# Two column units of a mixer output projection become one block with two seven-product chunk pairs

## The reference, cut to what matters

```python
oa = _mixer_sgu(za, ...)          # feature columns 0 to 511
ob = _mixer_shortconv(zb, ...)    # 512 to 1023
oc = _mixer_conformer(zc, ...)    # 1024 to 1535
od = _mixer_pool(zd, ...)         # 1536 to 2047
h = h + jnp.concatenate([oa, ob, oc, od], axis=-1) @ w_out[i]
y = _rms(h, norm_ffn_g[i])
h = h + (silu(y @ w_gate[i]) * (y @ w_up[i])) @ w_down[i]
y = _rms(h, norm_ple_g[i])
h = h + sigmoid(y @ w_ple_gate[i]) * (p[i] @ w_ple_proj[i])
```

## Time and profile before

| | |
|---|---|
| Median of 3 runs | 1378.77 us (1378.66 to 1379.81) |
| The profiled execution's own time | 1378.55 us |
| Its span | 1376.8 us |
| PE busy | 1370.2 us, 6169 matmuls |
| DVE, ACT, POOL busy | 1155.0, 885.1, 150.6 us |
| Moved by DMA | 352.94 MB, 256 GB/s mean |

### The profile page before, as it was taken

How to read it: one execution, slowest core, us unless ns; L and a number is a source line. 1 busy time by engine, 2 the same in 40 slices (tenths; PEclk the granted TensorE clock), 3 DMA queues, 4 the chain that set the end, 5 groups by cost and what they waited for, 6 DMA issues and landing times.

```text
span 1376.8 us, 16935 instructions
## 1 busy us (share of the span) xinstructions
PE 1370.2 (100%) x6169; PEld 1122.3 (82%) x6169; DVE 1155.0 (84%) x1332; ACT 885.1 (64%) x1181; POOL 150.6 (11%) x129
## 2 busy tenths in 40 slices
PE   9999999999999999999999999999999999999998
PEld 7888888888888888788888888888888887777887
DVE  6589986688999988899999889988766769886898
ACT  7476755576777555677756576756666656675564
POOL 2000010011111000110100011100000134430000
PEclk9999999999999999999999999999999999999999
DMA  9777658887999788899987889988987878889585
GB/s 331 251 211 212 203 164 277 278 248 242 292 283 261 229 260 257 252 270 266 281 267 249 252 252 244 281 292 236 326 297 274 279 240 259 254 271 300 193 251 170
DMA packets 183148, 352.94 MB, mean 256 GB/s; under 512 B 13106, under 2 KB 37934, under 8 KB 182937
## 3 DMA queue, kind: packets, MB, share of 16 engines
q1 hardware_dynamic: 160408, 291.66, 64.1%
q0 software_dynamic: 9568, 35.02, 13.0%
q10 hardware_dynamic: 13088, 25.18, 6.0%
HBM read 296.19 MB, written 27.31 MB: 235 GB/s over the span
## 4 chain that ended last, share of the span: by engine, by line
PE 96%; DVE 2%; DMA 1%; issue 1%; ACT 0%; POOL 0%; POOLq 0%; ACTq 0%; DVEq 0%
PE acc L2207 14%; PE acc L2209 14%; PE acc L2208 14%; PE acc L2388 13%; PE acc L2390 13%; PE acc L2391 13%; PE sp L2388 2%; PE tp L2390 2%; PE tp L2388 2%; PE tp L2391 2%; PE sp L2390 2%; PE sp L2391 2%; DMA wide<-w_raw 1%; PE acc L2269 1%; PE sp L2508 1%; DVE w_lo L1410 1%
## 5 line engine op out<-in xcount | busy, mean ns | idle before, releaser
L970 ACT ACTIVATE w_hi<-w_raw 128x1024 fp32r<-128x1024 f32 x451 | 472.0, 1056 | 298.5 <-PE acc L2209 192.1
L1410 DVE TENSOR_TENSOR w_lo<-w_raw,w_hi 128x1024 fp32r<-128x1024 f32 x429 | 519.8, 1226 | 137.1 <-ACT w_hi L970 134.5
L2207 PE MATMUL acc<-w_lo,hh 128*128 128x512 f32 x480 | 189.0, 394 | 0.0
L2209 PE MATMUL acc<-w_hi,hl 128*128 128x512 f32 x480 | 186.9, 389 | 0.0
L2208 PE MATMUL acc<-w_hi,hh 128*128 128x512 f32 x480 | 186.9, 389 | 0.0
L2388 PE MATMUL acc<-w_lo,yh 128*128 128x512 f32 x452 | 176.1, 390 | 0.0
L2391 PE MATMUL acc<-w_hi,yl 128*128 128x512 f32 x452 | 175.9, 389 | 0.0
L2390 PE MATMUL acc<-w_hi,yh 128*128 128x512 f32 x452 | 175.9, 389 | 0.0
L970 ACT ACTIVATE w_hi<-wide 128x1024 fp32r<-128x1024 f32 x108 | 114.4, 1060 | 72.8 <-DVE wide L1424 34.1
L1410 DVE TENSOR_TENSOR w_lo<-wide,w_hi 128x1024 fp32r<-128x1024 f32 x108 | 131.5, 1223 | 14.0 <-ACT w_hi L970 13.7
L2207 PE MATMUL acc<-w_lo,yh 128*128 128x512 f32 x352 | 137.4, 390 | 0.0
(11 more groups left out here) (333 smaller groups left out, 2225.8 us busy)
## 6 DMA issues: line engine op xcount, KB each, us to landing
w_raw<-in_w_gate SPq DMA_DIRECT2D x88, 512.0 KB, 5.7
w_raw<-in_w_up SPq DMA_DIRECT2D x88, 512.0 KB, 6.6
w_raw<-in_w_down SPq DMA_DIRECT2D x88, 512.0 KB, 6.5
w_raw<-in_w_in SPq DMA_DIRECT2D x64, 512.0 KB, 4.6
wide<-w_raw POOLq DMA_DIRECT2D x54, 512.0 KB, 6.0
w_raw<-in_swa_w_in ACTq DMA_DIRECT2D x48, 512.0 KB, 5.1
w_raw<-in_w_out SPq DMA_DIRECT2D x32, 512.0 KB, 5.8
w_raw<-in_w_ple_gate SPq DMA_DIRECT2D x32, 512.0 KB, 6.1
```

What stands on the lines that cost most here:

```text
L970: act.activation(w_hi[:, v % SPL], src, ACT.Copy).then_inc(hi_ready, 1)
L1410: dve.tensor_tensor(w_lo[:, v % SPL], src, w_hi[:, v % SPL].bitcast(F32), ALU.subtract).then_inc(lo_ready, 1)
L2207: pe.matmul(dst, xh[:, f, tk], w_lo[:, v % SPL, k], start=(f == 0), stop=False)
L2209: last = pe.matmul(dst, xl[:, f, tk], w_hi[:, v % SPL, k], start=False, stop=(f == CK * end + CK - 1))
```

## The change

The first two column units of `w_out` (units 12 and 13) become one `Block`, `MIXED_PAIR`, of 20 steps: twelve plain chunks and two quads (chunk pairs 0 and 1). With it come:

- a sum of the activations of those chunks, `whole_first` and `sum_h(0)`, in `tile[4]`, whose split takes the first of now five rounds of `h_sums` (all later rounds count one up);
- the four parkings of the projection of `p`, which now stand behind the loads 7, 8, 9 and 10 of the block, the first and the second of them around `move(T_OA)`, since `copy_tops` of the block is now the first of the program;
- other places for the residual's transposes, squares and `sum_y` in the last two units, which stay plain.

```diff
+MIXED_PLAN = plain(0, 2, 3) + plain(1, 2, 3) + plain(0, 6) + quad("g", 0) + plain(1, 6) + quad("g", 1) + plain(0, 7)
+MIXED_PLAN += plain(1, 7) + quad("u", 0) + quad("t", 0) + quad("s", 0) + quad("u", 1) + plain(0, 4) + quad("t", 1)
+MIXED_PLAN += quad("s", 1) + plain(0, 5) + plain(1, 4, 5)
+MIXED_AT = dict(whole=1, sums=4, sums_high=7, sums_low=8, m1=14, mix=18, mixed_gate=19, bank=19,
+                copied={6: [0], 7: [1]}, summed={0: 9, 1: 13})
...
+MIXED_PAIR = Block(OUT_UNIT, MIXED_PLAN, **MIXED_AT)
```

```diff
@@ SP
-            for j in range(NG):
+            b = MIXED_PAIR
+            for i, p in enumerate(b.loads):
+                role = int(p[0] == "u" or p[:2] == ("n", 1))
+                load(b.raw + i, wout_v, OUT_ROWS[p[-1]], CW * role)
+                if i == 7:
+                    put(T_OA)
+                if i == 8:
+                    fetch(T_OA)
+                if i in (7, 8, 9, 10):
+                    put_proj(i - 7)
+            for j in range(2, NG):
                 for c in range(8):
-                    if (j, c) == (0, 7):
-                        move(T_OA)
-                    if j >= 2 and c == 4:
+                    if (j, c) in ((2, 7), (3, 5)):
                         move(T_FFN + j - 2)
-                    if (j, c) in ((1, 3), (1, 7), (2, 7), (3, 3)):
-                        put_proj(((1, 3), (1, 7), (2, 7), (3, 3)).index((j, c)))
@@ ACT
+            b = MIXED_PAIR
+            for i in range(len(b.plan)):
+                for q in b.at["copied"].get(i, ()):
+                    copy_tops(b, q)
+                split_high(b.v0 + i)
...
+                if i == 3:
+                    turned_high(T_OA, hh[:, 8:12])
+                if i == b.at["sums_high"]:
+                    h_sums_to_high(0)
+                if i == b.at["m1"]:
+                    copy_m1(b)
@@ DVE
+            b = MIXED_PAIR
+            for i in range(len(b.plan)):
+                split_low(b.v0 + i)
...
+                if i == b.at["whole"]:
+                    whole_first()
...
+                if i == 3:
+                    turned_low(T_OA, hl[:, 8:12], hh[:, 8:12])
+                if i == b.at["sums"]:
+                    wait_half(dve, H_CN + 1)
+                    sum_h(0)
+                if i == b.at["sums_low"]:
+                    h_sums_to_low(0)
+                if i == b.at["mix"]:
+                    mix(b)
+                if i == b.at["mixed_gate"]:
+                    add_mixed_gate(b, 0)
+                if i == b.at["bank"]:
+                    add_bank(b, 0, 1)
...
+                    if (j, c) == (2, 0):
+                        wait_left(dve, OUT_UNIT)
+                        turn(T_FFN, columns(0))
+                        add_mixed_up(MIXED_PAIR, 1)
+                    if (j, c) == (2, 2):
+                        add_bank(MIXED_PAIR, 1, 2)
@@ PE
+            def before_mixed(i, p):
...
+                if p == ("n", 0, 6):
+                    pe.wait_ge(mix_ready, 2)
+                if p == ("g", 0):
+                    wait_half_left(pe, H_CN + 1)
+                    pe.wait_ge(oa_ready, 1)
+                if p == ("u", 0):
+                    pe.wait_ge(h_sums_low, 1)
+                if p == ("n", 0, 4):
+                    pe.wait_ge(turned_lo, T_OA + 1)
+            block(MIXED_PAIR, hh, hl, h_sums_hi, h_sums_lo, None, before_mixed)
```

More of the change, by code:

```diff
@@ L1127, in _, with copy_m1, h_sums_to_high @@
             take(PROJ_UNIT, wide_v[:, :, 0:CW], ACT.Copy, 1.0)
-            for j in range(NG):
+            def copy_m1(b):
+                act.wait_ge(used, b.split("g", b.quads[-1]) + 1)
+                if b is PAIR[0]:
+                    act.wait_ge(y_sums_low, 1)
+                act.activation(gates[:, 0], tp[0][:], ACT.Copy).then_inc(m1_copied, 1)
+            def h_sums_to_high(r):
+                act.wait_ge(h_sums, 4 * r + 4)
+                act.activation(h_sums_hi[:], h_wide(r), ACT.Copy).then_inc(h_sums_high, 1)
@@ new lines, in _ @@
+            b = MIXED_PAIR
[3 more added lines that the diff above has]
+                split_high(b.v0 + i)
+                if i < 3:
+                    take(PROJ_UNIT + 1 + i, wide_v[:, :, CW * (i + 1):CW * (i + 2)], ACT.Copy, 1.0)
+                if i == 2:
+                    wait_half_left(act, H_PO + 1)
+                    for h in range(2):
+                        wait_half(act, H_CN + h)
+                        for k in range(2):
+                            f = 2 * h + k
+                            last = act.activation(feat(6)[:, f], half_tile(H_CN + h)[:, k], ACT.Silu,
+                                                  bias=vec[:, V_LB + f:V_LB + f + 1],
+                                                  scale=vec[:, V_LG + f:V_LG + f + 1])
+                        last.then_inc(tp_left["a"], 1)
+                    wait_half_left(act, H_CN + 1)
+                    act.activation(hh[:, 12:16], feat(6), ACT.Copy).then_inc(mix_hi, 1)
+                if i == 3:
[4 more added lines that the diff above has]
+                    copy_m1(b)
@@ L1167, in hidden_high @@
                 turned_high(T_HID + m, hh[:, q:q + 4])
-            def copy_m1(b):
-                act.wait_ge(used, b.split("g", b.quads[-1]) + 1)
-                if b.no == 1:
-                    act.wait_ge(y_sums_low, 1)
-                act.activation(gates[:, 0], tp[0][:], ACT.Copy).then_inc(m1_copied, 1)
             def gate(m):
@@ new lines, in add_bank, with whole_first @@
+            def add_bank(b, d, after):
+                wait_unit(dve, b.unit + d % 2)
+                dve.wait_ge(mixed_added, after)
+                dve.tensor_tensor(columns(d), acc_pair[(b.unit + d) % 2][:], columns(d), ALU.add).then_inc(left["d"], 1)
+            def whole_first():
+                dve.tensor_tensor(tile[7][:], hh[:, 0:4].bitcast(F32).rearrange("p k n -> p (k n)"),
+                                  hl[:, 0:4].bitcast(F32).rearrange("p k n -> p (k n)"), ALU.add).then_inc(first_whole, 1)
@@ L1719, in _ @@
+                    if (j, c) == (3, 3):
+                        add_resid(OUT_UNIT + 2, 2)
+                    if (j, c) in ((2, 5), (3, 2)):
+                        ffn_turned_low(j - 2)
+                    if (j, c) in ((2, 5), (3, 4)):
+                        wait_left(dve, OUT_UNIT + j - 1)
+                        turn(T_FFN + j - 1, columns(j - 1))
+                    if j == 3 and c in (4, 5, 6):
+                        for i in {4: (0,), 5: (1, 2), 6: (3, 4)}[c]:
                             sum_y(i)
@@ L2352, in _ @@
                     to_features(H_CN, tok(4))
-            for j in range(NG):
-                for i in range(8):
-                    u, c = OUT_UNIT + j, i if j else OUT_FIRST[i]
-                    if j == 0 and c == 0:
-                        pe.wait_ge(mix_ready, 1)
-                        wait_half_left(pe, H_PO + 1)
-                    if j == 0 and c == 4:
-                        pe.wait_ge(turned_lo, T_OA + 1)
-                    if j == 0 and c == 6:
-                        pe.wait_ge(mix_ready, 2)
-                    chunk(START[u] + i, u, c, hh, hl, end=None if j else OUT_FIRST[-1])
             def third_sums_of(q, f):
@@ L2434, in block @@
                         last.then_inc(used, 1)
+            def before_mixed(i, p):
+                if i == 0:
+                    pe.wait_ge(mix_ready, 1)
+                    wait_half_left(pe, H_PO + 1)
+                if p == ("n", 0, 6):
[8 more added lines that the diff above has]
+            block(MIXED_PAIR, hh, hl, h_sums_hi, h_sums_lo, None, before_mixed)
+            for j in range(2, NG):
+                for c in range(8):
+                    chunk(START[OUT_UNIT + j] + c, OUT_UNIT + j, c, hh, hl)
             def pair(m):
```

215 lines of the change are left out of this document (90 added, 125 removed).

## The result

The changed kernel takes 1383.12 us (median of 7 runs, 1382.84 to 1384.42) against 1378.66 of the kernel before, measured beside it (7 runs, 1378.1 to 1379.81). The ratio is 1.0032, 95% interval 1.0022 to 1.0041: 4.5 us slower. 1381.0 was forecast, with 1378.0 to 1384.0 as the range. The profiled execution took 1382.97 us, 1381.2 of it the span.

A forecast was written before the change was run, and what follows sets the result against it. PE was taken as the bound (busy 1370.2 of 1376.8 us, 96% of the chain). Six fewer matmuls and the stall gave -1.36 + 3.55 = +2.2 us on 1378.77, so 1381.0; range 1378.0 to 1384.0.

The forecast's parts named there:

- Minus 1.36 for six matmuls: In the `w_out` stage, two quads take 6 fewer matmuls than four plain chunks, at 0.227 us each: 1.36 us saved.
- DVE's and ACT's added work at 0, at most 0.8: Activation sums before the sixth low split, 0 to 0.5 us; border to the third unit, 0 to 0.3; both taken as 0.
- The read back of `T_OA`: Four reads behind the write, issued from 207.40, taken to end at about 211.6 to 212; no loss priced.
- none elsewhere in the stage: Expected sign: a PE wait of about 3.5 us before the block's seventh step and no other in the stage.
- The fourth parking at 219.5: Landing of the last projection parking, for which ACT's first quad copy waits: 219.5, with bounds 217.9 and 222.4.
- one lost microsecond: Allowance for a slow start of the transfers behind the write of `T_OA`, included in the fourth parking's 219.5.
- From the landing to PE 3.4 us: From the fourth parking's landing through ACT's copy and split and DVE's split: 3.4 us, PE's seventh step at 222.9.
- The stall at 3.55 us: PE's wait before the block's seventh step: wanted at 219.35, got at 222.9; bounds 1.95 to 6.45 us.
- The rival with the clock: PE's clock falls to half in the seventh step's stall, costing 1.6 us more: +3.8, 1382.6; chance 0.31.
- Later effects at 0: Behind the seventh step, ACT's splits stay ahead and the first quad's accumulating DMA costs 0, up to 1 us.
- the parkings were not hidden: Rival that the parkings are hidden: all four land by 216, ACT isn't late; -1.4 to -0.9, about 1377.6; chance 0.17.
- the drain ended at 220.7 and not at 222.4: Rival of a spreading backlog: drain until 222.4 or accumulating DMA 1 us late, clock falls too; +6.7, 1385.5; chance 0.05.

The follow-up runs named there:

- e1: Changed kernel with SP's order alone altered: parkings 0 to 2 issued before the write of `T_OA`, parking 3 behind its read back; 1378.45 us, ratio 0.9999.
- e7: e1 with T_FFN+1's way through DRAM two loads earlier and one addition of the mixed bank later in DVE's order; 1378.07 us, ratio 0.9996.
- e4: Changed kernel with ten spare 512-column matmuls before PE's wait at the fifth step; 1384.61 us, ratio 1.0044.
- e3: Changed kernel with parkings 1 and 2 issued before the write of `T_OA`, parking 0 and a load before its read back, parking 3 behind; 1382.67 us.
- e9: e3 with T_FFN+1's write and read two loads earlier in SP's order; 1381.14 us, ratio 1.0019.
- e8: Changed kernel with T_FFN+1's write and read two loads earlier in SP's order; 1383.40 us, ratio 1.0031.
- e2: Changed kernel with all four parkings behind the read back of `T_OA`; 1387.20 us, ratio 1.0062.
- e6: Kernel before, without the block, given only the changed kernel's order of transfers around the read back of `T_OA`; 1382.59 us, ratio 1.0028.
- e10: e5 with T_FFN+1's write and read two loads earlier in SP's order; 1380.70 us, ratio 1.0014.
- e5: e3 with ten spare 512-column matmuls before PE's wait at the fifth step; 1382.67 us, ratio 1.0032.

## Why the prediction came out as it did

1383.12 us lies 0.9 below the upper end of the range, and the loss was twice what was forecast (+4.5 for +2.2). The range held it partly by luck. The wait for the parkings was foreseen and real, but the first and largest wait had no term in the sum; the total stayed inside only because the two causes reach nearly the same point.

**Minus 1.36 for six matmuls: held in the stage.** 6163 matmuls, and 0.92 to 1.20 us off the stage where PE didn't wait in the block (e1, e7). In the whole time it isn't told from nothing.

**DVE's and ACT's added work at 0, at most 0.8: held.** The four sums ran at 217.7 to 219.3, in the shadow of the stall. At the border 0.28 us were lost, within the 0 to 0.3 given. DVE was busy 14.7 us longer, for some 15.

**The read back of `T_OA`: this step failed.** The prediction had it land by 211.6 to 212 and priced it at nothing. It put parking 0 and a load in front of the reads and counted them for parking 3's sake only. It also had the fifth split end at 215.0, and four plain chunks end at 204.37 + 4 x 2.72 = 215.3: a margin of 0.2 to 0.3 us, in the prediction's own numbers, that was never set against the reads. They came 2.8 us later (214.35 for 211.56), and PE lost 2.6. In "none elsewhere in the stage" the forecast was wrong by its largest single wait.

**The fourth parking at 219.5: 1.2 us too early.** It landed at 220.7, inside the bounds of 217.9 to 222.4. The rate at the end was right: from 214.3 five transfers took 6.4 us, 1.28 each. What was mis-sized is the start, "one lost microsecond". From 207.4 to 214.3 the engines moved 1.8 x 274 + 3.8 x 253 + 1.3 x 399 = 1,970 KB, which at 400 GB/s is 4.9 us; it took 6.9, so two were lost. The Trainium skill ("DMA: Bandwidth & Descriptors", "Anatomy of one DMA — SWDGE (gpsimd) path") prices a transfer at a fixed 2 us and then 436 GB/s. The prediction's estimate by it took the 436 GB/s alone, without the fixed part, and was the farther off: 217.0 for 220.7. The same section of the Trainium skill says that the DMA engines wait on no semaphore and just consume their queues. For the queues the trace agrees, since the four reads landed at 212.3 to 214.3, behind parking 0 (209.3) and around the load (213.1) that stood in front of them; on the semaphores no run here tells.

**From the landing to PE 3.4 us, the seventh step at 222.9: held, at 224.13.** The chain took 3.3 to 3.4 (220.7 to 224.1); the 1.2 us are the landing's.

**The stall at 3.55 us: too small, and wrong in kind.** Against an undisturbed 219.3 (204.32 + 13.62 + 1.36), the seventh step came 4.8 us late, of which only 0.39 is a wait there. The rest had been lost before: 2.62 by standing and 1.8 by matmuls at the lower clock. e4 shows that parking 3 would have held PE to that time anyway, and e3 and e9 that the late reads cost nearly as much without parking 3 (stages of 91.11 and 90.31 for 91.00). Because the two causes reach nearly as far, their losses don't add, and the stage's 3.84 us stayed at the rival's +3.8, 1.6 above the forecast's +2.2. With the 0.61 of the rest (0.53 lost at 298, 0.3 at 391.55, the remainder scatter) the profiled execution comes to 1378.55 + 4.4 = 1383.0.

**The rival with the clock: it happened, in another place.** Its number (1382.6) is the nearest of all. It was worked for a stand before the seventh step and a half clock at 220 to 228; the fall came at 218.5, behind the fifth step. Its number is near by chance, since this price, 1.0 to 2.2 estimated and 1.7 to 2.1 seen in e9, is hidden in the changed kernel by parking 3. The Trainium skill ("TensorE: Matmul & The Clock Gate", "HAM oscillation — how this bites in real kernels") has a long idle gap throttle PE each time it comes. In the profiled runs the trace agrees for stands of 2.6, 2.7, 2.7, 3.3 and 6.3 us (changed, e8, e9, e3, e2), all of which ended at half clock, and one of 2.3 us (e6) did not. "Each time" doesn't hold over the other runs: by their mean clock six of e9's eleven and three of e3's ten had no fall. One reading under this rival was wrong, without effect on its price: the clock of the kernel before was not full from the start. Its 128-column matmuls start 0.21 us apart until 6.3 us and 0.11 apart from 7.6.

**Later effects at 0: nearly.** 0.53 us were lost at 298 behind the reads of T_FFN+1, and 0.3 at 391.55 behind DVE. The other rivals fall: the parkings were not hidden, the drain ended at 220.7 and not at 222.4, and the accumulating DMA cost nothing.

What stays open: the difference between the stage's gain and that of the whole time, in e1 (0.92 for 0.06) and e7 (1.20 for 0.65). 0.3 us of it are the gap at 386 to 392, behind DVE; what in DVE's order makes it was not tried, and the remainder is no larger than the scatter. Nor is it known which of the two transfers in front of the reads, parking 0 or the load, makes them late: every order here that has one has both.

## What to carry to other kernels

Before transfers are put in front of a round trip through DRAM, work out the margin of its last read to the engine that needs it, not only that of the transfers you move: here it was about 0.2 us, and 1 MB ahead of it cost 2.8. When two waits reach the same point, undoing one gives nothing, so test each alone, and look for the next wait downstream that would absorb the gain before pricing either. A queue's idle time just ahead of the work (here 200 to 204.5) is the place for writes whose source is already there: with its parkings there the same change lost nothing, though it gained nothing that could be measured either.

## What was not expected of the hardware

- Reads back of 128 KB each in a mix with loads move 253 GB/s at a DMA share of 1.03, where loads and parkings together move 399 to 407.
- The fall of TensorE's clock is not certain for stands of 2.3 to 3.3 us. By the mean granted clock the same program (e9, profiled stand 2.7 us) ran six times at full clock and five times with a fall, 2.1 us apart in their medians. One profiled stand of 2.3 us left it full (e6); stands of 2.6 us and 3.3 us were each followed by half clock for 3.4 us, one of 6.3 us by half clock for 6.8.
- Ten spare matmuls in a wait kept the clock full in every run of e10 (11 of 11), and gained what not falling gains. That was nothing where a later wait was bound by a transfer (e4, e5).
